# Expert blocks in another order, a ring of 24 half-size pieces, and first products that wait input by input

## What is computed

```python
def hybrid_layer(x, c, ...):                      # two layers
    mod = (c @ w_ada + b_ada)[:, None, :]
    h = rms_norm(x) * (1 + sc_m) + sh_m
    x_lru, q_down, kv_down, k_rope, gate_a, gate_b = jnp.split(h @ w_in, IN_SPLIT_POINTS, axis=-1)
    y_a = rg_lru(causal_depthwise_conv(x_lru, conv_w, conv_b), ...)
    y_b = mla(q_down, kv_down, k_rope, ..., w_uq, w_ukv)
    y = jax.nn.sigmoid(gate_a) * y_a + jax.nn.sigmoid(gate_b) * y_b
    x = x + g_m * (y @ w_out)
    h = rms_norm(x) * (1 + sc_f) + sh_f
    gate, up = jnp.split(h @ w_ffn_in, 2, axis=-1)
    return x + g_f * ((jax.nn.silu(gate) * up) @ w_ffn_out)

def moe_ffn(h, ...):                              # second block, 32 experts, top 4
    top_vals, top_idx = lax.top_k(xt @ w_router + b_router, 4)
    ...                                           # per token and chosen expert e:
    gate = jnp.minimum(xb @ w_gate[e] + b_gate[e], 7.0)
    up = jnp.clip(xb @ w_up[e] + b_up[e], -7.0, 7.0)
    y = (gate * jax.nn.sigmoid(1.702 * gate) * (up + 1.0)) @ w_down[e] + b_down[e]
    # weighted by the softmax of the four values and summed per token
```

## Time and profile before

| | us |
|---|---|
| median of 3 runs | 3100.54 (3099.65 to 3103.19) |
| the profiled execution's own time | 3100.72 |
| its span, first to last instruction | 3099.0 |
| first gc to last gc (50 blocks) | 1842.8 to 3028.0 |
| PE busy | 2829.5, 91% |
| DVE / ACT busy | 1233.7 / 743.8 |
| mean granted TensorE clock | 0.966 |

### The profile page before, as it was taken

How to read it: one execution, slowest core, us unless ns; L and a number is a source line. 1 busy time by engine, 2 the same in 40 slices (tenths; PEclk the granted TensorE clock), 3 DMA queues, 4 the chain that set the end, 5 groups by cost and what they waited for, 6 DMA issues and landing times.

```text
span 3099.0 us, 36173 instructions
## 1 busy us (share of the span) xinstructions
PE 2829.5 (91%) x13128; PEld 1715.6 (55%) x13128; DVE 1233.7 (40%) x2127; ACT 743.8 (24%) x1068; POOL 112.6 (4%) x171
## 2 busy tenths in 40 slices
PE   7897899999999998999999978999989999998984
PEld 5685678888777667788777742333322333332321
DVE  5864667665673454333385431111111111111113
ACT  4724332122373433222233310000000000000001
POOL 0020000000000000000010000000000000000001
PEclk8999999999999999999999979999999999999997
DMA  8273246764323022242223089584799899989994
GB/s 252 81 249 91 69 121 172 217 177 130 109 71 94 13 68 82 66 118 81 89 69 101 1 307 409 196 324 151 288 410 410 327 366 410 396 314 410 410 410 184
DMA packets 393037, 638.65 MB, mean 206 GB/s; under 512 B 28448, under 2 KB 278432, under 8 KB 392944
## 3 DMA queue, kind: packets, MB, share of 16 engines
q1 hardware_dynamic: 374832, 590.77, 53.3%
q0 software_dynamic: 9376, 31.14, 2.9%
q10 hardware_dynamic: 8736, 15.47, 1.4%
HBM read 610.78 MB, written 26.54 MB: 206 GB/s over the span
## 4 chain that ended last, share of the span: by engine, by line
PE 71%; SPq 8%; DVE 7%; DMA 6%; ACT 5%; issue 3%; POOL 0%; ACTq 0%; DVEq 0%; another core or an unknown queue 0%
PE bank L2444 25%; PE bank L193 12%; PE bank L195 12%; PE bank L194 12%; SPq L2334 6%; DMA ring<-w_down 4%; PE bank L2449 1%; PE bank L1048 1%; DVE WLO L166 1%; PE bank L1049 1%; SPq L315 1%; DMA ring<-w_gate 1%; PE bank L2436 1%; PE bank L1089 1%; ACT WHI L156 1%
## 5 line engine op out<-in xcount | busy, mean ns | idle before, releaser
L2444 PE MATMUL bank<-ring,xT 128*64 128x512 f32 x3200 | 718.3, 595 | 43.6 <-DMA ring<-w_gate 21.4
L193 PE MATMUL bank<-HH,WHI 128*128 128x512 f32 x1344 | 543.1, 404 | 23.2 <-DVE HL L602 14.8
L195 PE MATMUL bank<-HH,WLO 128*128 128x512 f32 x1344 | 528.1, 393 | 0.0
L194 PE MATMUL bank<-HL,WHI 128*128 128x512 f32 x1344 | 527.8, 393 | 0.0
L2444 PEld LDWEIGHTS bank<-ring,xT 128*64 128x64 f32 x3200 | 220.4, 137 | 491.0 <-issue 385.0
L2444 PE MATMUL bank<-ring,hT 128*64 128x512 f32 x1600 | 361.7, 597 | 27.4 <-DMA ring<-w_down 25.7
L166 DVE TENSOR_TENSOR WLO<-RAW,WHI 128x2048 fp32r<-128x2048 f32 (+1 forms) x132 | 281.6, 2135 | 135.3 <-ACT WHI L156 135.1
L193 PEld LDWEIGHTS bank<-HH,WHI 128*128 128x128 f32 x1344 | 255.2, 190 | 92.4 <-issue 16.9
L194 PEld LDWEIGHTS bank<-HL,WHI 128*128 128x128 f32 x1344 | 255.5, 190 | 54.1 <-issue 3.4
L195 PEld LDWEIGHTS bank<-HH,WLO 128*128 128x128 f32 x1344 | 255.0, 190 | 54.8
L156 ACT ACTIVATE WHI<-RAW 128x2048 fp32r<-128x2048 f32 (+1 forms) x132 | 234.4, 1776 | 204.2 <-PE bank L195 160.2
(11 more groups left out here) (426 smaller groups left out, 2819.1 us busy)
## 6 DMA issues: line engine op xcount, KB each, us to landing
ring<-w_gate SPq DMA_DIRECT2D x128, 1024.0 KB, 12.5
ring<-w_up SPq DMA_DIRECT2D x128, 1024.0 KB, 14.1
ring<-w_down SPq DMA_DIRECT2D x128, 1024.0 KB, 15.9
RAW<-w_ffn_in SPq DMA_DIRECT2D x88, 512.0 KB, 5.2
RAW<-w_ada SPq DMA_DIRECT2D x40, 1024.0 KB, 5.3
RAW<-w_in SPq DMA_DIRECT2D x37, 1024.0 KB, 6.2
RAW<-w_ffn_out SPq DMA_DIRECT2D x32, 704.0 KB, 4.8
expert_results<-ysb ACTq DMA_DIRECT2D x102, 128.0 KB, 5.5
```

The lines of the kernel that those rows point to most:

```text
L193: pe.matmul(out, lhi, rhi, start=start, stop=False)
L194: pe.matmul(out, lhi, rlo, start=False, stop=False)
L195: return pe.matmul(out, llo, rhi, start=False, stop=stop)
L2444: ins = pe.matmul(out[halves(h), :], xT[:, k % 4, halves(k // 4)], m["ring"][:, c, at:at + 512], start=False, stop=k == KD - 1)
```

## The change

- The order of chunks is ukv, uq 0, uq 1. uq 1 is prepared on ACT and DVE at the start of the attention pipeline's second step (h = -1).
- `arriving` waits input by input and does both output groups for each input. It is used for lru 0 of layer 1, and for out 0 and fi 0 of both layers. The first fo group waits for ffl piece by piece.
- The q and kv statistics stand behind ga 1; in layer 0 modulation column 0 is added with column 1, behind ga 0.
- The zero rows are written after ffl 1 of layer 1. `scans` stands behind qk 3, at v 0.
- The ring has 24 pieces of 512 KB. The bytes are the same.
- The experts are ordered by their counts: expert 0 stays first, the next 11 in falling order stand at places 1, 4, 7 to 31, and the other 20 fill the places between from the last to the first. The routing gets the steps for this: two more exchanges between DVE and PE, and other small operations in place of the old.

```diff
@@ -96,7 +97,7 @@
-    out += [("uq", 0), ("uq", 1), ("ukv", 0)]
+    out += [("ukv", 0), ("uq", 0), ("uq", 1)]
...
     for n, (kind, i, _) in enumerate(W_CHUNKS):
-        if kind == "uq":
+        if kind == "ukv":
             break
...
-    feed(W_INDEX["ukv", 0])
...
     for h in range(-2, HEADS):
+        if h == -1:
+            feed(W_INDEX["uq", 1])
...
     def ada_columns(kind, i):

         r = L.ada_after.get((kind, i))
-        if r is None:
+        if r is None or (kind, i) == ("kv", 0):
             return
         which, chunk = L.ada[r]
-        if which == "own" and r == 0:
+        if which == "own" and r == 1:
             pe.wait_ge(*sg.event("act_out", ("lru_tanh", 3)))
+            ada_column(0)
+        ada_column(r)
+
+    def ada_column(r):
+
+        which, chunk = L.ada[r]
         pe.wait_ge(*sg.event("ada_acc", r))
         for j in range(2):
             c = 2 * chunk + j
             ins = pe.matmul(b[7 if which == "own" else 6][:, c:c + 1], m["acc"][:, r % 2, j * P:(j + 1) * P], one[:, 0:1], start=True, stop=True)
...
+    def arriving(kind, i, event, number, xh=HH, xl=HL):
+
+        n, g = W_INDEX[kind, i], FIRST_GROUP[kind, i]
+        hi, lo = weights(n)
+        outs = [bank(g), bank(g + 1)]
+        for k in range(KD):
+            pe.wait_ge(*sg.event(event, number(k)))
+            for j in range(2):
+                c = k * 256 + j * P
+                ins = split3(pe, outs[j][:], hi[:, c:c + P], lo[:, c:c + P], xh[:, k, :], xl[:, k, :], k == 0, k == KD - 1)
+                if k == KD - 1:
+                    ins.then_inc(*sg.inc("pe_step", also=[("acc", g + j), *([("w_used", n)] if j else [])]))
         ada_columns(kind, i)
...
         for i in range(4):
-            dense("lru", i, norm=None if i else 0)
             if i:
+                dense("lru", i)
                 gates(i - 1)
+            else:
+                arriving("lru", 0, "hl", lambda k: (0, k))
...
     dense("ga", 0)
+    dense("ga", 1)

     pe.wait_ge(*sg.event("act_sq", "qkv"))
     pe.matmul(b[4][:], one, m["sq2"][:, 0, :], start=True, stop=False)
     pe.matmul(b[4][:], one, m["sq2"][:, 1, :], start=False, stop=True)
     pe.matmul(b[5][:], one, m["ti"][:, 0, :], start=True, stop=True).then_inc(*sg.inc("pe_step", also=[("stat", "qkv")]))
-    dense("ga", 1)
...
-    pe.wait_ge(*sg.event("yl", KD - 1))
-    for i in range(4):
+    arriving("out", 0, "yl", lambda k: k, m["yh"], m["yl"])
+    for i in range(1, 4):
...
-            dense("fi", half * NF + j, norm=None if half or j else 1)
+            if half or j:
+                dense("fi", half * NF + j)
+            else:
+                arriving("fi", 0, "hl", lambda k: (1, k))
         for j in range(KD):
             i = half * KD + j
             n, g = W_INDEX["fo", i], FIRST_GROUP["fo", i]
             hi, lo = weights(n)
             out = bank(g)
-            pe.wait_ge(*sg.event("ffl", half * NF + NF - 1))
             for k in range(NF):
+                if j == 0:
+                    pe.wait_ge(*sg.event("ffl", half * NF + k))
                 c = k * P
...
-                eng.wait_ge(*layers[0].sg.event("kp"))
+                eng.wait_ge(*layers[1].sg.event("ffl", 1))
                 zero_results(eng, MIN_BLOCKS + 1, MAXB - MIN_BLOCKS)
...
+def expert_order():
+
+    e = np.arange(EXPERTS)
+    tie = np.where(e == 0, 8.0 * S, -e / 64)
+    full = (EXPERTS - 2) // 3 + 1
+    place = np.zeros(EXPERTS)
+    place[1:full + 1] = 1 + 3 * np.arange(full)
+    place[full + 1:] = np.setdiff1d(e[1:], place[1:full + 1])[::-1]
+    v = np.zeros((P, N_ORD), np.float32)
+    v[:, 0:32], v[:, 32:64] = tie, place
+    v[0:32, 64], v[0:32, 65], v[0:32, 66] = tie, e, -e
+    return v
...
                 if i == 0:
                     forget()
-                if i == 2:
-                    scans()
+            elif kind == "v" and not i:
+                scans()
...
-MOE_SLOTS = 12
+MOE_SLOTS = 24
...
-MOE_CHUNKS = [(w, c) for w in ("gate", "up", "down") for c in range(4)]
+MOE_CHUNKS = [(w, k) for w in ("gate", "up", "down") for k in range(KD)]
+UP_FROM, DOWN_FROM = KD, 2 * KD
...
+                         (m["ord"][:], W["consts"][0:32, K_ORD:K_ORD + N_ORD])):
...
-            if c == MOE_SLOTS - 1:
+            if c == MOE_SLOTS - 2:
...
-        v.tensor_copy(m["cntc"][:], b[6][0:32, 160:161]).then_inc(*sg.inc("ro_step"))
+        cntc, nbc, nbf, keyc, pos, order = m["cntc"][:], m["nbc"][:], m["nbf"][:], m["keyc"][:], m["pos"][:], m["ord"][:]
+        grid = m["grid"][:]
+
+        v.tensor_tensor(grid, b[6][0:32, P:P + 32], order[:, 0:32], ALU.add)
+        v.tensor_scalar(keyc, b[6][0:32, 160:161], order[:, 64:65], None, ALU.add)
+        v.tensor_copy(cntc, b[6][0:32, 160:161]).then_inc(*sg.inc("ro_step"))
         v.wait_ge(*sg.last("ro_step"))
-        v.tensor_scalar(m["nbc"][:], m["cntc"][:], 1.0 / BLK, UP, ALU.mult, ALU.add).then_inc(*sg.inc("ro_step"))
+        v.tensor_scalar(grid, grid, keyc, None, ALU.is_gt)
+        v.tensor_scalar(nbc, cntc, 1.0 / BLK, UP, ALU.mult, ALU.add).then_inc(*sg.inc("ro_step"))
         v.wait_ge(*sg.last("ro_step"))
-        v.tensor_scalar(m["nbf"][:], m["nbc"][:], MAGIC, -MAGIC, ALU.add, ALU.add).then_inc(*sg.inc("ro_dve", also=[("nbc", None)]))
+        v.tensor_reduce(pos, grid, AX.X, ALU.add)
+        v.tensor_scalar(nbf, nbc, MAGIC, -MAGIC, ALU.add, ALU.add).then_inc(*sg.inc("ro_step"))
+        v.wait_ge(*sg.last("ro_step"))
+        v.scalar_tensor_tensor(grid, m["i32"][0:32, :], pos, order[:, 32:64], ALU.is_equal, ALU.mult).then_inc(*sg.inc("ro_step"))
+        v.wait_ge(*sg.last("ro_step"))
+        v.tensor_reduce(pos, grid, AX.X, ALU.add).then_inc(*sg.inc("ro_dve", also=[("place", None)]))
         v.tensor_copy(rk, b[6][:, 0:P])
-        v.tensor_copy(cnt, b[6][:, P:P + 32]).then_inc(*sg.inc("ro_step"))
+
+        v.wait_ge(*sg.event("places"))
+        v.tensor_scalar(grid, b[5][0:32, 208:240], pos, None, ALU.is_gt).then_inc(*sg.inc("ro_dve", also=[("ahead", None)]))
+
+        v.wait_ge(*sg.event("firsts"))
+        v.tensor_copy(keyc, b[5][0:32, 200:201])
+        v.tensor_tensor(nbc, b[5][0:32, 200:201], nbf, ALU.add).then_inc(*sg.inc("ro_step"))
         v.wait_ge(*sg.last("ro_step"))
-        v.tensor_scalar(nb, cnt, 1.0 / BLK, UP, ALU.mult, ALU.add).then_inc(*sg.inc("ro_step"))
-        v.wait_ge(*sg.last("ro_step"))
-        v.tensor_scalar(nb, nb, MAGIC, -MAGIC, ALU.add, ALU.add).then_inc(*sg.inc("ro_step"))
-        v.wait_ge(*sg.last("ro_step"))
-        v.tensor_tensor_scan(incl, one[:, 0:32], nb, 0.0, ALU.mult, ALU.add).then_inc(*sg.inc("ro_step"))
-        v.wait_ge(*sg.last("ro_step"))
-
-        v.wait_ge(*sg.event("inclc"))
-        v.tensor_copy(m["nbc"][:], b[5][0:32, 200:201]).then_inc(*sg.inc("ro_step"))
-        v.wait_ge(*sg.last("ro_step"))
-        v.tensor_scalar(m["cmp"][:], m["i48"][0:32, :], m["nbc"][:], None, ALU.is_ge).then_inc(*sg.inc("ro_dve", also=[("cmp", None)]))
+        v.tensor_scalar(m["cmp"][:], m["i48"][0:32, :], keyc, None, ALU.is_ge)
+        v.tensor_scalar(m["cmp2"][:], m["i48"][0:32, :], nbc, None, ALU.is_ge).then_inc(*sg.inc("ro_dve", also=[("cmp", None)]))
+        v.tensor_copy(excl, b[6][:, 192:224])
         v.wait_ge(*sg.event("bep"))
+        v.tensor_copy(be, b[5][:, 256:256 + NB + 1]).then_inc(*sg.inc("ro_step"))
...
-        pe.wait_ge(*sg.event("nbc"))
-        pe.matmul(b[5][0:32, 200:201], m["tri"][0:32, 0:32], m["nbf"][:], start=True, stop=True).then_inc(*sg.inc("ro_pe", also=[("inclc", None)]))
+        pe.wait_ge(*sg.event("place"))
+        pe.matmul(b[5][0:32, 208:240], m["pos"][:].broadcast_to([32, 32]), ident[0:32, 0:32], start=True, stop=True)
+        pe.matmul(b[5][0:1, 244:245], m["nbf"][:], one[0:32, 0:1], start=True, stop=True).then_inc(*sg.inc("ro_pe", also=[("places", None)]))
+        pe.wait_ge(*sg.event("ahead"))
+        pe.matmul(b[5][0:32, 200:201], m["grid"][:], m["nbf"][:], start=True, stop=True)
+        pe.matmul(b[6][:, 192:224], m["nbf"][:].broadcast_to([32, P]), m["grid"][:], start=True, stop=True).then_inc(*sg.inc("ro_pe", also=[("firsts", None)]))
         pe.wait_ge(*sg.event("cmp"))
-        pe.matmul(b[5][:, 256:256 + NB + 1], one[0:32, :], m["cmp"][:], start=True, stop=True).then_inc(*sg.inc("ro_pe", also=[("bep", None)]))
+        pe.matmul(b[5][:, 256:256 + NB + 1], m["ord"][:, 65:66].broadcast_to([32, P]), m["cmp"][:], start=True, stop=False)
+        pe.matmul(b[5][:, 256:256 + NB + 1], m["ord"][:, 66:67].broadcast_to([32, P]), m["cmp2"][:], start=False, stop=True).then_inc(*sg.inc("ro_pe", also=[("bep", None)]))
...
-    a = MOE_CHUNKS[c][1]
-    return sp.dma_start(m["ring"][:, c, :].rearrange("p (k n) -> p k n", k=2), w[:, 2 * a:2 * a + 2, :])
+    return sp.dma_start(m["ring"][:, c, :], w[:, MOE_CHUNKS[c][1], :])
...
-        loads(i, "bei", "fresh", range(0, 8))
-        loads(i, "bed", "freshd", range(8, 12))
+        loads(i, "bei", "fresh", range(0, DOWN_FROM))
```

(23 more changed lines are left out.)

30 lines of the change are left out of this document (16 added, 14 removed).

## The result

The kernel after the change takes 3006.91 us in the median of four runs (3004.80 to 3008.36), the kernel before, run beside it, 3101.80 (3099.65 to 3103.19): a ratio of 0.9694, with a 95% interval of 0.9677 to 0.9711. The forecast was 3004.5, between 2986 and 3036. The profiled execution took 3008.36 with a span of 3006.6, so against the profiled one of before (3100.72) 92.4 us are gone. The sum had 96.2.

What follows compares the result with a forecast made beforehand. PE was taken as the bound, busy 91% of the span with 71% of the chain, so time falls only where it waits or runs at low clock. Terms summed to -96.2 from 3100.72, giving 3004.5 us, range 2986 to 3036.

Steps and rivals of the forecast that it cites:

- the loop: Expert loop, first to last gc: new expert order and half-size ring pieces cut PE's starvation from 93.2 us, -39.
- scans: Mixer: moving the scans behind qk 3 shortens PE's wait at v 0 from 5.61 to about 1.4 us, -4.2.
- the statistics: Layers: q and kv statistics behind ga 1 cost +0.5 us in layer 1 and +2.0 in layer 0, +2.5.
- fi with lru: fi 0 of both layers and layer 1's lru 0: both output groups for each input as it arrives, -10.1 us.
- ukv: Attention in both layers: ukv first and zero rows moved let V start earlier, uq 1 prepared later, -20.3 us.
- routing: Before the first expert block: more small DVE steps and two more exchanges for the new order, +1.8 us.
- fo: First fo groups: the wait for the last ffl, 11.8 us idle, goes, with 1.6 for the clock, -13.4.
- less 2.2: 2.9 each: Expert loop: half-size pieces cut each of five runs of three loads behind large experts from 5.1 to 2.9 us.
- out 0: First out products, both layers: taking inputs one by one removes the wait for all eight yl, -13.5 us.
- A: Rival, expert loop: a run of three loads costs 8.0 us wherever it stands, -13 instead of -39: 3030; chance 0.12.
- B: Rival, layers: the next wait replaces the removed one, losing half of the -59 outside the experts: 3034; chance 0.14.
- D: Rival, expert loads: half-size transfers each cost something, at 0.4 us the loop gets +129: 3172; chance 0.03.

Runs made afterwards that it cites:

- order12: The kernel after with 12 ring pieces of 1 MB instead of 24 half-size ones, new expert order kept: 3006.58 us, first to last gc 1154.7.
- zeros_layer0: The kernel after with the zero rows written after kp of layer 0 again, ukv still first: 3014.24 us.
- uq_first: The kernel after with chunk order uq 0, uq 1, ukv, all prepared ahead of V, zero rows still in layer 1: 3021.93 us.
- stats_early: The kernel after with the q and kv statistics again between ga 0 and ga 1, modulation column 0 behind kv: 3006.35 us.
- waits_as_before: The kernel after with the old waits at out 0, fo, fi 0 and layer 1's lru 0 put back together: 3047.12 us.
- rows_2k: The kernel after with 512 KB transfers each holding half the columns of two slices, rows of 2 KB for 4 KB: 3063.92 us.

## Why the prediction was right, point by point

The time lies 2.4 us above the forecast, and every term but the expert loop's within 1.5 us of its size. Part of this closeness is luck: in the profiled execution the terms that fell short (the loop 5.1, scans 1.3, the statistics and fi with lru 0.9) are half made up by what the sum didn't have or had too small (ukv 1.2, routing and fo 0.8, the 1.5 in no term).

- **Starvation as a count of loads.** The term that carried the loop was right in its mechanism: 9.6 us behind for each single-block expert, traffic-bound behind two-block experts (7.6 forecast and measured, in five runs). The step that was mis-sized is the one on half-size pieces: "less 2.2: 2.9 each". Between `order12` and the kernel after they gave 1.0 a run (4.9 to 3.9 in the mean), not 2.2, and in other executions of the same loop one run behind a large expert went up to 5.2. Why half pieces give less than half a load and half a use is not settled; neither is the 1.5 us that they cost at the start, for which the sum had nothing. These two are the whole miss of the loop: the stalls were forecast at 52.5 and came to 59.1, of which 5.0 are the five runs behind large experts (19.5 for 14.5) and 1.5 the start.
- **ukv first.** The cause was named rightly, with both of its halves; that neither half alone is enough was not said, and `zeros_layer0` and `uq_first` showed it. Preparing uq 1 later costs 0.4 a layer, not 1.1; that it lies partly beside the first scores is the likely reason, not tested alone. V of layer 0 began at 238.95 and not at 236, since the statistics' 2.7 us come ahead of it.
- **Waits for all of the inputs.** out 0 and fo came out within 0.4 us, and with fi 0 and lru 0 put back together they cost 41 us. The clock was part of it: layer 0's out 0 gained 8.4 for a wait of 6.40, and its first product now takes 0.47 for 0.80.
- **Input by input.** The pace of the inputs (1.42 us for two times three matmuls) was the bound, with the low clock in the first of them, as forecast: -3.5, -3.9 and -2.4.
- **Statistics.** In layer 1 one wait took the other's place, read from two end times 0.5 us apart in the earlier trace rows. In layer 0 the size came out by luck: the prediction's +2.0 was for K's path getting later, but the first score follows V's start by 11.03 us in the kernel after and in `stats_early` alike; the 2.7 us lie ahead of V, at ga 1. The edit loses 3 us, and undoing it gains them.
- **Scans.** 2.9 for 4.2, and a wait of 4.17 left at v 0 where the prediction had 1.4: it took the whole duration of the removed work, and didn't ask what DVE would wait for next. The answer stood in its own timeline, where WLO follows the rounding of the same chunk on ACT.
- **The rivals.** A and B were ruled out by the loop's stalls and by `waits_as_before`. D was wrong for halves of 1 MB with rows of 4 KB, but was closer than it looked: the same halving done across the columns (`rows_2k`) costs 53 us.

## What to carry to other kernels

Where a ring is fed for items of unequal work, count the loads between two items that have work to spare: here a run of two loads costs nothing, one of three 4 to 9 us and one of five 24, and single-block experts behind the last load cost nothing. An engine that waits for all of its inputs before the first product can be given them one at a time, and here the gains of all such places added up. When work is moved off an engine's path, take as its gain not the work's duration but the distance to the next thing that this engine will wait for.
